# A hybrid decoder layer on one core: the last two experts scattered singly by products of 64 rows, ten loads of one unit, and a final norm by whole blocks

## The chip, the core and the metric

The kernel runs on one core of a Trainium2 chip. The metric is the device time of one execution in microseconds; each figure is the median of several runs. Engines are named as in the profile: PE (TensorE, matrix products) with its weight loads PEld, DVE (VectorE), ACT (ScalarE), POOL (GpSimd), SP (SyncE, which here issues nearly all DMAs).

## The reference

One layer, batch 1, 256 tokens of width 1024, all in float32. It is cut here to what bears on the change, which lies wholly in the expert part and the final norm.

```
def moe_ffn(x, w_router, b_router, w_gu, b_gu, w_down, b_down):
    logits = (x @ w_router + b_router)
    top_vals, top_idx = lax.top_k(logits, TOP_K)          # 4 of 32
    top_w = jax.nn.softmax(top_vals, axis=-1)
    gates = jnp.sum(jax.nn.one_hot(top_idx, N_EXPERTS) * top_w[..., None], axis=1)
    def expert(acc, params):
        wgu_e, bgu_e, wd_e, bd_e, gate_e = params
        h = x @ wgu_e + bgu_e                              # 1024 -> 2048
        hg, hu = h[:, :D_FF], h[:, D_FF:]
        hg = jnp.minimum(hg, 7.0); hu = jnp.clip(hu, -7.0, 7.0)
        act = (hu + 1.0) * (hg * jax.nn.sigmoid(1.702 * hg))
        return acc + gate_e[:, None] * (act @ wd_e + bd_e), None

h = x + (attention heads | Conformer convolution) @ w_out
h = h + moe_ffn(rmsnorm(h, norm_ffn_g), ...)
out = rmsnorm(h, norm_final_g)      # y = h * rsqrt(mean(h*h) + 1e-6) * g
```

## The kernel before

The first tenth of the time is attention, convolution, output projection and routing. Then come 32 experts in a loop that is unrolled, and at last the norm.

**Weights.** An expert has 12 units of 1 MB: 8 of `w_gu` (up projection, 128 input rows each) and 4 of `w_down` (256 rows each, two rows of 1024 numbers on each partition). They lie in a ring of 22 units in SBUF. `SEQUENCE` gives their order: expert by expert, but for the last two experts (numbers 30 and 31) first all up units of 30, all up units of 31, then the down units of 30, then those of 31. `load_sizes` packs them into DMAs: four units mostly; from expert 30 on (`FINE_FROM`) two, and the very last two singly. SP issues a load as soon as PE has counted `units_used` up far enough to free its place, and PE waits on a semaphore of `load_full` for each load, at its first unit.

**One expert.** For each expert up to 64 of the 256 tokens are gathered (`gather`) by products with a 0/1 matrix. `up` multiplies them with the up units; an output of 64 rows takes half of the array's columns, so the two halves of each weight row go side by side (128\*64 in the profile). DVE and ACT make the activation (`expert_pass`, `gate_sigmoid`), PE turns it (`turn_act`), `down` multiplies with the down units. The result is 64 tokens by 1024, held in PSUM as two halves of 512 columns one above the other: partitions 0 to 63 the first half, 64 to 127 the second.

**Scattering.** Experts go in pairs. The results of the even one are copied to partitions 0 to 63 of `y_sb`, those of the odd one to 64 to 127 (`copy_results`). DVE writes each token's gate in a matrix (`weigh_tokens`), PE turns it (`turn_weights`), ACT copies it to `scatter_sb` (`copy_scatter`), and `scatter(buffer, t, h)` adds a pair's results to the block of 128 tokens t and half of columns h of `resid`, which lies in PSUM; these are four products of 128 rows for each pair, spread over the next two experts. For the last pair nothing comes behind: `last_expert` runs `up`, two scatters of the pair before with `turn_weights` between them, the down projection of expert 30 with `turn_act` of 31 in its middle, then that of 31. Behind it ACT and DVE copy one half each, and all four scatters follow.

**The norm.** For each block and each half, ACT squares and sums (L557), DVE multiplies with the gain (L1161) and makes the mean of the two sums in two small steps (L1165, L1168), ACT takes the root, DVE the reciprocal (L1172). The scaling of block 0 is POOL's, in two halves (L547); that of block 1 is DVE's (L1176) and ACT's (L800). SP issues four stores in the order (0,0), (0,1), (1,0), (1,1). There is a path for experts with over 64 tokens (`extra`); the inputs used here don't take it.

The order of each engine's work is the program's text; engines meet by semaphores alone.

## Time and profile before

| | us |
|---|---|
| median of 3 runs | 1042.81 |
| lowest, highest | 1042.51, 1043.61 |
| span of the profiled execution, first to last instruction | 1041.7 |
| PE busy | 1000.4 (96%) |
| DVE busy | 238.4 (23%) |
| ACT busy | 144.9 (14%) |
| POOL busy | 16.5 (2%) |
| HBM read | 419.82 MB, 404 GB/s over the span |

The profiled execution's time by the clock of the runs is not listed apart; its span stands 1.1 us below the median of the runs. In the profile a float32 product appears as two records, so four products are "x8". Matmul records overlap each other: from the start of one row to the start of the next is a better measure than the sum of the durations. L1182 is the line of the helper that issues every product; what a row does is told by its tiles: `work<-ring,main` is up or down projection, `work<-select,main` gathering, `resid<-main` scattering, L1538 turning an activation, L1496 turning weights. A bracket at the end is the idle time in front and what ended it.

### The profile page before, as it was taken

What the parts mean: (1) busy time and instruction counts of PE and PEld (TensorE: products, weight loads), DVE (VectorE), ACT (ScalarE), POOL (GpSimd) and SP (SyncE); (2) the same over time, 40 slices, a digit from 0 to 9 for tenths busy, and PEclk for the clock granted to TensorE, in tenths of its full rate; (3) what the DMA queues carried; (4) which work ended last, traced back from release to release, by engine and by line L of the source; (5) the groups of instructions that cost most, each with busy time, mean ns of one, the idle gap of its engine ahead of it and who ended that gap; (6) DMA issues with size and microseconds to landing.
All of it is one profiled execution on the core that took longest, in us unless ns stands there. A gap on an engine that the chain in (4) does not pass through costs nothing.

```text
span 1041.7 us, 12870 instructions
## 1 busy us (share of the span) xinstructions
PE 1000.4 (96%) x5774; PEld 411.0 (39%) x5775; DVE 238.4 (23%) x535; ACT 144.9 (14%) x277; POOL 16.5 (2%) x28
## 2 busy tenths in 40 slices
PE   9999999999999999999999999899999999999996
PEld 7875544333333333333333333332333333323332
DVE  3995341111011111111111111110111111101121
ACT  5144320100000101010101001000101001000102
POOL 4000000000000000000000000000000000000001
PEclk9999999999999999999999999999999999999999
DMA  9995599999999999999999999999999999999993
GB/s 308 392 414 195 214 397 399 416 418 424 430 424 434 429 433 427 431 427 435 425 433 427 433 427 433 427 435 428 428 433 427 432 430 430 432 428 426 425 424 161
DMA packets 33381, 421.75 MB, mean 405 GB/s; under 512 B 4031, under 2 KB 8427, under 8 KB 14380
## 3 DMA queue, kind: packets, MB, share of 16 engines
q1 hardware_dynamic: 31772, 420.57, 96.0%
q8 instruction: 47, 0.77, 0.3%
q10 hardware_dynamic: 1552, 0.33, 0.2%
q14 instruction: 10, 0.08, 0.0%
HBM read 419.82 MB, written 1.05 MB: 404 GB/s over the span
## 4 chain that ended last, share of the span: by engine, by line
PE 62%; DMA 36%; DVE 1%; issue 1%; POOL 0%; POOLq 0%; ACT 0%; SPq 0%; DVEq 0%
PE work L1182 53%; DMA ring<-in_w_gu 32%; PE resid L1182 7%; DMA ring<-in_w_down 4%; PE work L1538 1%; PE work L1298 0%; PE work L1496 0%; PE work L1397 0%; POOLq L148 0%; DVE main L938 0%; POOL main L547 0%; PE work L1208 0%; DVE ring L837 0%; DVE main L918 0%; DVE main L1161 0%
## 5 line engine op out<-in xcount | busy, mean ns | idle before, releaser
L1182 PE MATMUL work<-ring,main 128*64 128x512 f32 (+1 forms) x3080 | 685.3, 598 | 28.7 <-DMA ring<-in_w_gu 25.8
L1182 PEld LDWEIGHTS work<-ring,main 128*64 128x64 f32 (+1 forms) x3080 | 222.3, 139 | 472.4 <-issue 431.5
L1091 DVE TENSOR_SCALAR main<-work 128x512 f32<-128x512 f32 x32 | 22.1, 691 | 582.7 <-PE work L1182 582.7
L734 ACT ACTIVATE main<-main 128x512 f32<-128x512 f32 x32 | 20.2, 631 | 459.0 <-DVE main L1091 459.0
L1182 PE MATMUL work<-ring 128*128 128x256 f32 (+2 forms) x308 | 71.9, 403 | 1.8 <-DVE ring L837 0.9
L1182 PE MATMUL resid<-main 128*128 128x512 f32 x128 | 68.1, 618 | 0.9 <-DVE main L1153 0.9
L1182 PE MATMUL work<-bgu_rows,ident 128*64 128x512 f32 (+1 forms) x260 | 62.4, 599 | 0.0
L1182 PEld LDWEIGHTS work<-ring 128*128 128x128 f32 (+1 forms) x308 | 55.6, 186 | 16.4 <-issue 8.3
L1182 PEld LDWEIGHTS work<-select,main 128*128 128x128 bf16 x1536 | 46.7, 98 | 26.6 <-issue 26.3
L748 ACT ACTIVATE main<-work 64x512 f32<-64x512 f32 x63 | 37.2, 591 | 118.7 <-PE work L1182 117.9
L1182 PE MATMUL work<-select,main 128*128 128x64 bf16 x1536 | 50.7, 193 | 0.1
L1084 DVE TENSOR_SCALAR lent<-count,place,gates 128x64 f32<-128x64 f32 x64 | 16.9, 308 | 146.9 <-PE work L1496 139.1
L884 DVE SCALAR_TENSOR_TENSOR main<-ring,main 128x256 f32<-128x256 f32 x116 | 46.6, 478 | 1.3 <-ACT main L609 1.2
L739 ACT ACTIVATE main<-work 128x512 f32<-128x512 f32 x32 | 19.1, 597 | 115.1 <-PE work L1538 115.1
L1098 DVE SCALAR_TENSOR_TENSOR main<-main 128x512 f32<-128x512 f32 x32 | 34.1, 1067 | 1.1
L1182 PEld LDWEIGHTS resid<-main 128*128 128x128 f32 x128 | 19.4, 189 | 27.4 <-issue 27.4
L1182 PE MATMUL resid<-ring,main 128*128 128x512 f32 (+1 forms) x68 | 28.8, 571 | 0.0
L1095 DVE TENSOR_TENSOR main<-main 128x512 f32<-128x512 f32 x32 | 22.2, 693 | 5.4 <-ACT main L734 5.4
L1182 PEld LDWEIGHTS work<-bgu_rows,ident 128*64 128x64 f32 x260 | 15.6, 135 | 19.4 <-issue 17.7
L1538 PEld LDWEIGHTS work<-ident,main 128*128 128x128 f32 x128 | 15.8, 141 | 17.9 <-issue 17.0
L745 ACT ACTIVATE main<-work 128x256 f32<-128x256 f32 x16 | 6.1, 383 | 114.7 <-PE work L1496 114.7
L1092 DVE TENSOR_SCALAR main<-work 128x512 f32<-128x512 f32 x32 | 21.8, 680 | 0.0
(190 smaller groups left out, 275.0 us busy)
## 6 DMA issues: line engine op xcount, KB each, us to landing
ring<-in_w_gu SPq DMA_DIRECT2D x36, 4096.0 KB, 41.8
ring<-in_w_gu SPq DMA_DIRECT2D x36, 2048.0 KB, 17.1
ring<-in_w_down SPq DMA_DIRECT2D x18, 4096.0 KB, 43.5
ring<-in_w_gu SPq DMA_DIRECT2D x8, 3072.0 KB, 37.7
ring<-in_w_down SPq DMA_DIRECT2D x11, 2048.0 KB, 15.7
ring<-in_w_down SPq DMA_DIRECT2D x20, 1024.0 KB, 14.3
ring<-in_w_gu SPq DMA_DIRECT2D x15, 1024.0 KB, 27.6
ring<-in_w_down SPq DMA_DIRECT2D x4, 3072.0 KB, 40.0
```

The source lines that it names most:

```text
L734: nc.scalar.activation(sig_h, gate_h, ACT.Sigmoid, scale=SWIGLU_ALPHA).then_inc(sig_ready, 1)
L739: nc.scalar.activation(to, work[:, act_bank(n), :], ACT.Copy).then_inc(act_t_ready, 1)
L745: nc.scalar.activation(scatter_sb[buffer][0:rows, :], work[0:rows, TURN_BANK, 0:TB * P], ACT.Copy).then_inc(scatter_ready, 1)
L748: return nc.scalar.activation(y_sb[buffer][h][parity * CAP:(parity + 1) * CAP, :], work[h * CAP:(h + 1) * CAP, bank, :], ACT.Copy)
L884: V.scalar_tensor_tensor(acc, u_pad[:, c, j:j + SEQ], dw_cols[:, c, j:j + 1], acc, ALU.mult, ALU.add)\
L1084: done = V.tensor_scalar(weighted[:, t, parity * CAP:(parity + 1) * CAP], count[:, bass.ds(r * CAP, CAP)], place[:, t, bass.ds(e, 1)], gat ...
L1091: V.tensor_scalar(gate_h, work[:, GATE_BANK, :], SWIGLU_LIMIT, None, ALU.min).then_inc(gate_clamped, 1)
L1092: V.tensor_scalar(up_h, work[:, UP_BANK, :], SWIGLU_LIMIT, -SWIGLU_LIMIT, ALU.min, ALU.max).then_inc(up_clamped, 1)
L1095: V.tensor_tensor(sig_h, sig_h, gate_h, ALU.mult).then_inc(glu_ready, 1)
L1098: V.scalar_tensor_tensor(gate_h.rearrange("p (b j) -> p j b", b=4), up_h.rearrange("p (j b) -> p j b", b=4), 1.0, sig_h.rearrange("p (j b) ...
L1182: return nc.tensor.matmul(out_, lhsT, rhs, start=start, stop=stop, skip_group_check=True)
L1538: last = nc.tensor.transpose(work[:, act_bank(n), j * P:(j + 1) * P], gate_h[:, j * P:(j + 1) * P], ident[:, :])
```

## The change

Four things change, all from the last two experts on.

1. **Loads.** From unit 374 on (the last two up units of expert 31 and all eight down units of 30 and 31) each load is one unit. The very last unit is split in two DMAs, one for each of its two rows, with a semaphore for the second (`last_row_in`).
2. **Scattering singly.** Experts 30 and 31 each have a scatter matrix of their own. DVE writes the same weights in both halves of the matrix (`weigh_tokens` with parity 0 and 1), so that after the turn they stand on partitions 0 to 63 and on 64 to 127. The result is copied as it lies, one copy of 128 partitions by ACT, and `scatter_alone` adds it in products of 64 rows: half h of the columns from partitions 64h to 64h+63. There are four such products for each of the two experts. DVE's copy of one half is gone.
3. **Order on PE.** The scatters of the pair before and the turn of weights go in the middle of the last up projection; a second turn of weights goes behind `turn_act` in the middle of expert 30's down projection; expert 30's four scatters go behind the first unit of expert 31's down projection.
4. **Norm.** ACT squares 1024 columns at once and takes the root with scale 1/1024 and the epsilon as bias (from a column that POOL sets at the start). Half 0 of each block is multiplied with the gain first and scaled afterwards (POOL for block 0, ACT for block 1); half 1 is done by DVE in one instruction for both factors. The stores go in the order (0,1), (0,0), (1,1) from SP, and (1,0) from ACT's own queue.

PE behind the fourth up unit of expert 31. `resid<-main` are the scatters, L1496 (after: L1508) the turn of weights, `load_full` the loads' semaphores. Before:

```order
L1182 MATMUL work<-ring,main 64x512 [waits load_full3]
L1182 MATMUL work<-ring,main 64x512 x7
L1182 MATMUL resid<-main 128x512 [waits scatter_ready,act_t_ready]
L1496 MATMUL work<-ident,lent 128x128 [waits weighted_ready]
L1496 MATMUL work<-ident,lent 128x128
L1182 MATMUL resid<-main 128x512
L1182 MATMUL work<-ring,main 64x512 [waits load_full4,act_t_ready]
L1182 MATMUL work<-ring,main 64x512 x7
```

and now:

```order
L1188 MATMUL work<-ring,main 64x512 [waits load_full1]
L1188 MATMUL work<-ring,main 64x512 x7
L1188 MATMUL resid<-main 128x512 [waits scatter_ready,act_t_ready]
L1188 MATMUL resid<-main 128x512
L1508 MATMUL work<-ident,lent 128x128 [waits weighted_ready]
L1508 MATMUL work<-ident,lent 128x128
L1188 MATMUL work<-ring,main 64x512 [waits load_full2]
L1188 MATMUL work<-ring,main 64x512 x7
```

The four instructions that stood behind the eighth up unit stand behind the fourth, and the two scatters are next to each other.

PE in the last down projection, expert 31's. Before, from its first unit to the end of its fourth and the first scatters:

```order
L1182 MATMUL work<-ring,main 64x512 [waits load_full6,act_t_ready]
L1182 MATMUL work<-ring,main 64x512 x7
L1182 MATMUL work<-ring,main 64x512 [waits load_full7]
L1182 MATMUL work<-ring,main 64x512 x3
L1182 MATMUL work<-ring,main 64x512 [waits load_full8]
L1182 MATMUL work<-ring,main 64x512 x3
L1182 MATMUL resid<-main 128x512 [waits y_ready,scatter_ready]
L1182 MATMUL resid<-main 128x512 [waits y_last]
L1182 MATMUL resid<-main 128x512 x2
```

and now, from behind its first unit:

```order
L1188 MATMUL resid<-main 128x512 [waits y_ready]
L1188 MATMUL resid<-main 128x512 x3
L1188 MATMUL work<-ring,main 64x512 [waits load_full10]
L1188 MATMUL work<-ring,main 64x512 x3
L1188 MATMUL work<-ring,main 64x512 [waits load_full11]
L1188 MATMUL work<-ring,main 64x512 x3
L1188 MATMUL work<-ring,main 64x512 [waits load_full12]
L1188 MATMUL work<-ring,main 64x512
L1188 MATMUL work<-ring,main 64x512 [waits last_row_in]
L1188 MATMUL work<-ring,main 64x512
L1188 MATMUL resid<-main 128x512 [waits y_ready,scatter_ready]
L1188 MATMUL resid<-main 128x512 x3
```

Four scatters of expert 30 stand between the first unit and the second (their rows read 128x512 by their output; they take 64 rows in), each unit has its own wait, the last one two, and the four scatters at the end wait once.

DVE in the final norm; L1161 (after: L1170) is the product with the gain. Before:

```order
L1161 TENSOR_TENSOR main<-resid,ring 128x512 [waits o_squared,final_gain_in]
L1165 TENSOR_SCALAR stat<-stat 128x1
L1168 TENSOR_SCALAR stat<-stat 128x1 [waits o_squared,o_mean]
L1161 TENSOR_TENSOR main<-resid,ring 128x512 [waits o_squared]
L1172 RECIPROCAL stat<-stat 128x1 [waits o_root]
L1161 TENSOR_TENSOR main<-resid,ring 128x512 [waits o_squared,o_scale]
L1165 TENSOR_SCALAR stat<-stat 128x1
L1168 TENSOR_SCALAR stat<-stat 128x1 [waits o_squared,o_mean]
L1161 TENSOR_TENSOR main<-resid,ring 128x512 [waits o_squared]
L1172 RECIPROCAL stat<-stat 128x1 [waits o_root]
L1176 TENSOR_SCALAR main<-main,stat 128x512 [waits o_gained,o_scale]
```

and now:

```order
L1170 TENSOR_TENSOR main<-resid,ring 128x512 [waits o_squared,final_gain_in]
L1175 RECIPROCAL stat<-stat 128x1 [waits o_root]
L1177 SCALAR_TENSOR_TENSOR main<-resid,stat,ring 128x512 [waits o_scale]
L1170 TENSOR_TENSOR main<-resid,ring 128x512 [waits o_squared]
L1175 RECIPROCAL stat<-stat 128x1 [waits o_root]
L1177 SCALAR_TENSOR_TENSOR main<-resid,stat,ring 128x512 [waits o_scale]
```

Eleven instructions become six; the two on single columns are gone, and half 1 is read from PSUM by one instruction with both factors.

The diff, without semaphore declarations, the waits on the constants, the path for full experts and the last counts:

```diff
+    ALONE_FROM, LAST_UNIT = UNITS * E - 10, UNITS * E - 1
...
-                sizes.append(1 if n >= UNITS * E - 2 else 2)
+                sizes.append(1 if n >= ALONE_FROM else 2)
...
+                    if first == LAST_UNIT:
+                        halves_ = ring_rows(first, size, from_.shape[1])
+                        sp.dma_start(halves_[:, 0, :], from_[:, 0, :]).then_inc(load_full[k % LOAD_SEMS], 16)
+                        sp.dma_start(halves_[:, 1, :], from_[:, 1, :]).then_inc(last_row_in, 16)
+                        continue
...
-            for n in range(HALVES):
-                t, half = n // 2, slice(n % 2 * HALF, (n % 2 + 1) * HALF)
-                if n < 2:
-                    sp.wait_ge(result_ready, n + 1)
-                else:
-                    sp.wait_ge((last_ready, last_half_ready)[n - 2], 1)
+            for t, h, made in ((0, 1, (last_ready, 1)), (0, 0, (result_ready, 1)), (1, 1, (last_ready, 2))):
+                half = slice(h * HALF, (h + 1) * HALF)
+                sp.wait_ge(*made)
...
+            def last_expert(e):
+                copy_scatter(PAIRS - 1, 1, P, (PAIRS - 2) * HALVES)
+                gate_sigmoid(e)
+                copy_act(e)
+                copy_scatter(PAIRS, 0, P, (PAIRS - 1) * HALVES)
+                act.wait_ge(units_used, downs_used(e - 1))
+                nc.scalar.activation(alone_y[0], work[:, OUT_BANK, :], ACT.Copy).then_inc(y_ready, 1)
...
-            copy_half((E - 1) // 2 % 2, (E - 1) % 2, 1, UP_BANK).then_inc(y_last, 1)
+            nc.scalar.activation(alone_y[1], work[:, UP_BANK, :], ACT.Copy).then_inc(y_ready, 1)
...
+            act.wait_ge(consts_ready, 6)
             for t in range(TB):
-                for h in range(2):
-                    act.wait_ge(scattered, total * (HALVES * (SEQ // CAP - 1)) + (HALVES * (PAIRS - 1) + 2 * t + h + 1))
-                    mean_square(resid[:, t, h * HALF:(h + 1) * HALF], work[:, GATE_BANK + h, :],
-                                stat[:, 2 * t + h:2 * t + h + 1], o_squared)
-                act.wait_ge(o_mean, 2 * t + 2)
-                nc.scalar.activation(stat[:, 8 + t:9 + t], stat[:, 6 + t:7 + t], ACT.Sqrt).then_inc(o_root, 1)
-                if t == TB - 1:
-                    act.wait_ge(o_scale, TB)
-                    act.wait_ge(o_gained, HALVES)
-                    nc.scalar.activation(result[:, t, HALF:D], result[:, t, HALF:D], ACT.Copy, scale=stat[:, 10 + t:11 + t])\
-                        .then_inc(last_half_ready, 1)
+                act.wait_ge(scattered, total * (HALVES * (SEQ // CAP - 1)) + (SCATTERS - HALVES + 2 * t + 2))
+                mean_square(resid[:, t, :], work[:, GATE_BANK:GATE_BANK + 2, :].rearrange("p h n -> p (h n)"), stat[:, t:t + 1], o_squared)
+                act.wait_ge(o_squared, t + 1)
+                nc.scalar.activation(stat[:, 8 + t:9 + t], stat[:, t:t + 1], ACT.Sqrt, scale=1.0 / D, bias=eps_col[:, :]).then_inc(o_root, 1)
+            act.wait_ge(o_gained, 2)
+            act.wait_ge(o_scale, TB)
+            nc.scalar.activation(result[:, 1, 0:HALF], result[:, 1, 0:HALF], ACT.Copy, scale=stat[:, 11:12]).then_inc(last_half_ready, 1)
+            act.wait_ge(last_half_ready, 1)
+            act.dma_start(out[0, P:2 * P, 0:HALF], result[:, 1, 0:HALF]).then_inc(result_out, 16)
...
+                if e >= E - 2:
+                    weigh_tokens(e, 0, 0, PAIRS - 1 + e - (E - 2))
+                    weigh_tokens(e, 0, 1, None)
+                elif e > 1:
...
-            V.tensor_copy(y_sb[(E - 1) // 2 % 2][0][CAP:P, :], work[0:CAP, UP_BANK, :]).then_inc(y_ready, 1)
...
-            def gained(t, h):
-                half = slice(h * HALF, (h + 1) * HALF)
-                dve.wait_ge(o_squared, 2 * t + h + 1)
-                V.tensor_tensor(result[:, t, half], resid[:, t, half], final_gain[:, half], ALU.mult).then_inc(o_gained, 1)
-            for t in range(TB):
-                gained(t, 0)
-                V.tensor_scalar(stat[:, 4 + t:5 + t], stat[:, 2 * t:2 * t + 1], 1.0 / D, RMS_EPS, ALU.mult, ALU.add).then_inc(o_mean, 1)
-                dve.wait_ge(o_mean, 2 * t + 1)
-                dve.wait_ge(o_squared, 2 * t + 2)
-                V.tensor_scalar(stat[:, 6 + t:7 + t], stat[:, 2 * t + 1:2 * t + 2], 1.0 / D, stat[:, 4 + t:5 + t], ALU.mult, ALU.add)\
-                    .then_inc(o_mean, 1)
-                gained(t, 1)
-                dve.wait_ge(o_root, t + 2)
+            def gained(t):
+                dve.wait_ge(o_squared, t + 1)
+                V.tensor_tensor(result[:, t, 0:HALF], resid[:, t, 0:HALF], final_gain[:, 0:HALF], ALU.mult).then_inc(o_gained, 1)
+            def finished(t):
+                dve.wait_ge(o_root, t + 1)
                 V.reciprocal(stat[:, 10 + t:11 + t], stat[:, 8 + t:9 + t]).then_inc(o_scale, 1)
                 dve.wait_ge(o_scale, t + 1)
-                if t == TB - 1:
-                    dve.wait_ge(o_gained, 2 * t + 1)
-                    V.tensor_scalar(result[:, t, 0:HALF], result[:, t, 0:HALF], stat[:, 10 + t:11 + t], None, ALU.mult).then_inc(last_ready, 1)
+                V.scalar_tensor_tensor(result[:, t, HALF:D], resid[:, t, HALF:D], stat[:, 10 + t:11 + t], final_gain[:, HALF:D],
+                                       ALU.mult, ALU.mult).then_inc(last_ready, 1)
+            for t in range(TB):
+                gained(t)
+                finished(t)
...
+            def scatter_alone(buffer, y, t):
+                for h in range(2):
+                    rows = slice(h * CAP, (h + 1) * CAP)
+                    mm(resid[:, t, h * HALF:(h + 1) * HALF], scatter_sb[buffer][rows, t * P:(t + 1) * P], y[rows, :], False, False).then_inc(scattered, 1)
...
+                        if n == LAST_UNIT and b == 1:
+                            pe.wait_ge(last_row_in, 16)
...
-                pair, before = e // 2, (e // 2 + 1) % 2
-                up(e, e)
-                pe.wait_ge(act_t_ready, e)
-                pe.wait_ge(scatter_ready, pair)
-                scatter(before, 1, 0)
-                pe.wait_ge(weighted_ready, e + 1)
-                turn_weights()
-                scatter(before, 1, 1)
-                down(e - 1, e - 1, between=lambda: turn_act(e))
-                down(e, e)
+                def during_up():
+                    pe.wait_ge(act_t_ready, e)
+                    pe.wait_ge(scatter_ready, PAIRS - 1)
+                    scatter(0, 1, 0)
+                    scatter(0, 1, 1)
+                    pe.wait_ge(weighted_ready, E)
+                    turn_weights()
+                def during_other_down():
+                    turn_act(e)
+                    pe.wait_ge(scatter_ready, PAIRS)
+                    pe.wait_ge(weighted_ready, E + 2)
+                    turn_weights()
+                def during_down():
+                    pe.wait_ge(y_ready, E - 1)
+                    for t in range(TB):
+                        scatter_alone(1, alone_y[0], t)
+                up(e, e, between=during_up)
+                down(e - 1, e - 1, between=during_other_down)
+                down(e, e, between=during_down, between_at=1)
...
-            scatter((PAIRS - 1) % 2, 0, 0)
-            pe.wait_ge(y_last, 1)
-            scatter((PAIRS - 1) % 2, 0, 1)
-            for h in range(2):
-                scatter((PAIRS - 1) % 2, 1, h)
+            for t in range(TB):
+                scatter_alone(0, alone_y[1], t)
```

## Rows read from the trace of the kernel before

**Rows 1.** Page, sections 1 and 2: engine shares, and GB/s in 40 slices.
```profile
PE 1000.4 (96%) x5774; PEld 411.0 (39%) x5775; DVE 238.4 (23%) x535; ACT 144.9 (14%) x277; POOL 16.5 (2%) x28
...
GB/s 308 392 414 195 214 397 399 416 418 424 430 424 434 429 433 427 431 427 435 425 433 427 433 427 433 427 435 428 428 433 427 432 430 430 432 428 426 425 424 161
```

**Rows 2.** Windows of 59 us: busy us by engine, granted clock, DMA share, GB/s.
```profile
830.00:889.00 59.00, 53.24 (x312) 19.57 (x312) 8.76 (x18) 5.20 (x9) 0.00 (x0) 0.97 1.00 428
...
959.00:1018.00 59.00, 58.92 (x344) 21.43 (x340) 11.48 (x20) 4.94 (x9) 0.00 (x0) 1.00 1.00 424
```

**Rows 3.** Timeline of PE, last 64 us: start us, us, engine, line, operation, count.
```profile
977.96 13.95 PE L1182 MATMUL work<-ring,main 128*64 128x512 f32 x64
...
997.57 14.26 PE L1182 MATMUL work<-ring,main 128*64 128x512 f32 x64
1011.75 1.12 PE L1182 MATMUL resid<-main 128*128 128x512 f32 x2
1012.72 0.38 PE L1496 MATMUL work<-ident,lent 128*128 128x128 f32 x2
1012.93 1.02 PE L1182 MATMUL resid<-main 128*128 128x512 f32 x2
1013.89 3.65 PE L1182 MATMUL work<-ring,main 128*64 128x512 f32 x16
1017.47 0.66 PE L1538 MATMUL work<-ident,main 128*128 128x128 f32 x4
1018.06 3.65 PE L1182 MATMUL work<-ring,main 128*64 128x512 f32 x16
1022.99 7.09 PE L1182 MATMUL work<-ring,main 128*64 128x512 f32 x32 [1.28 <-DMA ring<-in_w_down]
1030.95 3.67 PE L1182 MATMUL resid<-main 128*128 128x512 f32 x8 [0.87 <-DVE main L1153]
```

**Rows 4.** Timeline of PE's weight loads at two waits for data.
```profile
1018.05 0.20 PEld L1182 LDWEIGHTS work<-ring,main 128*64 128x64 f32 x4 [0.17 <-DMA ring<-in_w_down]
...
1027.82 0.14 PEld L1182 LDWEIGHTS work<-ring,main 128*64 128x64 f32 x2 [0.33 <-DMA ring<-in_w_down]
```

**Rows 5.** Timeline of DVE: last expert's activation, then the final norm.
```profile
1014.05 1.07 DVE L1098 SCALAR_TENSOR_TENSOR main<-main 128x512 f32<-128x512 f32 x1
1030.12 0.68 DVE L1153 COPY main<-work 64x512 f32<-64x512 f32 x1 [15.00 <-PE work L1182]
1032.87 0.69 DVE L1161 TENSOR_TENSOR main<-resid,ring 128x512 f32<-128x512 f32 x1 [2.07 <-ACT work L557]
...
1034.46 0.15 DVE L1172 RECIPROCAL stat<-stat 128x1 f32<-128x1 f32 x1
```

**Rows 6.** Timeline of ACT in the final norm.
```profile
1032.08 0.58 ACT L557 ACTIVATE work<-resid 128x512 f32<-128x512 f32 x1 [0.49 <-PE resid L1182]
1032.58 0.20 ACT L557 ACTIVATION_READ_ACCUMULATOR work<-resid 128x1 f32 x1
```

**Rows 7.** Timeline of POOL in the final norm.
```profile
1034.71 3.11 POOL L547 TENSOR_SCALAR main<-main,stat 128x512 f32<-128x512 f32 x2 [910.35 <-DVE stat L1172]
```

**Rows 8.** Timeline of SP: the last two stores issued.
```profile
1038.24 0.94 SPq L487 DMA_DIRECT2D result<-main  x2
```

**Rows 9.** Groups by form, PE: busy us, mean ns of one.
```profile
L1182 PE MATMUL resid<-spare,lent 32*128 32x512 f32 x8 | 3.7, 600 | 0.0
```

**Rows 10.** Groups by form, ACT.
```profile
L557 ACT ACTIVATE main<-main 128x1024 f32<-128x1024 f32 x1 | 1.1, 1057 | 9.2 <-DVE main L1019 9.2
```

**Rows 11.** Groups by form, DVE.
```profile
L970 DVE SCALAR_TENSOR_TENSOR main<-main,stat 128x1024 f32<-128x1024 f32 x1 | 1.3, 1285 | 1.3 <-ACT main L694 1.3
...
L970 DVE SCALAR_TENSOR_TENSOR main<-main,stat 128x384 f32<-128x384 f32 x2 | 1.1, 610 | 0.0
```

**Rows 12.** DMA issues: KB each, median us from issue to landing.
```profile
result<-main SPq DMA_DIRECT2D x4, 256.0 KB, 2.4
...
spare<-in_b_down ACTq DMA_DIRECT2D x1, 128.0 KB, 6.9
```

More of the change, by code:

```diff
@@ L500, in _ @@
             nc.gpsimd.memset(ones_b[:, :], 1.0).then_inc(consts_ready, 1)
+            nc.gpsimd.memset(eps_col[:, :], RMS_EPS).then_inc(consts_ready, 1)
             nc.gpsimd.memset(ident_b[:, :], 0.0).then_inc(consts_step, 1)
@@ L771, in extra @@
                 copy_act(o + E)
-                copy_scatter(o + PAIRS, 0, CAP, (o + PAIRS) * HALVES)
+                copy_scatter(o + ALONE_SETS, 0, CAP, (o + ALONE_SETS) * HALVES)
                 copy_results(o * UNITS + downs_used(E), 0, 0)
                 nc.scalar.activation(stat[:, 13:14], stat[:, 14:15], ACT.Sqrt)
-            for e in range(E):
+            for e in range(E - 1):
                 expert(e)
@@ L1511, in extra_bias, with up @@
                     mm(work[:, bank, :], extra_sel[:, bank, :, :].rearrange("p h c -> p (h c)"), bgu_rows[:, :], True, False)
-            def up(g, e, o=None):
+            def up(g, e, o=None, between=None):
                 if not (isinstance(g, int) and g == 0):
@@ L1517, in up @@
                 for kb in range(KB):
+                    if kb == KB // 2 and between is not None:
+                        between()
                     if isinstance(g, int) and g == 0:
@@ L1539, in turn_act, with down @@
                 last.then_inc(act_turned, 1)
-            def down(g, e, o=None, between=None):
+            def down(g, e, o=None, between=None, between_at=DOWN_UNITS // 2):
                 pe.wait_ge(act_t_ready, g + 1)
@@ L1544, in down @@
                 for u in range(DOWN_UNITS):
-                    if u == DOWN_UNITS // 2 and between is not None:
+                    if u == between_at and between is not None:
                         between()
@@ L1640, in _ @@
             last_expert(E - 1)
-            pe.wait_ge(scatter_ready, PAIRS)
+            pe.wait_ge(scatter_ready, PAIRS + 1)
             pe.wait_ge(y_ready, E)
-            scatter((PAIRS - 1) % 2, 0, 0)
-            pe.wait_ge(y_last, 1)
-            scatter((PAIRS - 1) % 2, 0, 1)
-            for h in range(2):
-                scatter((PAIRS - 1) % 2, 1, h)
+            for t in range(TB):
+                scatter_alone(0, alone_y[1], t)
             def extra(e, r, o):
```

36 lines of the change are left out of this document (17 added, 19 removed).

## The prediction, made before the changed kernel ran

> **What bounds the kernel now.** I read the page first: TensorE counts as busy for 96% of the span, and the weights arrive at about 430 GB/s in nearly every slice, so the two are close [rows 1]. Windows of 59 us come next. One near the middle of the expert loop has 53.2 us of TensorE work and a full DMA stream; the one before the end has 58.9 us of work and a full stream [rows 2]. So the stream sets the pace of the loop, but in the last two experts TensorE has hardly any slack of its own. The change touches only this end, so I then went along TensorE's timeline through its last 64 us [rows 3]. The granted clock is 1.00 in that last window and 0.97 in the other; the sum below holds at 1.00.
>
> There the reader is to see three things. The last expert's up projection begins at 997.57. From there to 1030.08 (the end of the last down product, 1022.99 + 7.09) TensorE works on without a break except for about 0.3 us inside the 14.26 us stretch (8 units at the rate of 13.95 for 8), 0.17 us before 1018.05 [rows 4], and 1.28 us before 1022.99, where it waits for a load of two units. And the last unit's data is waited for once more, until 1027.82 [rows 4], the very moment when TensorE comes to it (its weights are loaded just ahead of 1022.99 + 3 x 1.74 = 1028.2): in this run both limits meet there. Behind 1030.08 comes a serial tail: copies of the result, four scatter products (1030.95 to 1034.62) [rows 3], the norm, and stores. POOL normalises both halves of block 0 in 3.11 us, until 1037.82 [rows 7]; SP issues stores in program order, so block 1's two stores, ready earlier, are issued only behind it, the last at 1039.18 minus half of 0.94, about 1038.71 [rows 8]. The span ends 2.52 us after 1039.18. That tail of 11.6 us from 1030.08 is where time can be had.
>
> Span here is 1041.7, the median of three runs 1042.81: about 1.1 lies around the span, and I keep that.
>
> **The change part by part.**
>
> *Loads.* Units land one by one in the slowest queue's time: a two-unit load is waited for at 1022.99 and the last unit lands at 1027.82, two units later, so 2.4 us a unit. With single units the wait of 1.28 goes, and so do the 0.17 and the 0.3: by the landings so counted every unit is there at least 0.8 us before TensorE's new schedule (below) wants it. The last unit comes as two rows. If data were the limit, half a unit of products would be left behind 1027.82: 2.26 us (to 1030.08) less half of 1.74, so the last product would end at 1029.2. This is the floor. Smaller loads cost stream time: between windows with four-unit and with two-unit loads the rate falls from 428 to 424 GB/s [rows 2], 0.55 us in 59 us for about six more loads, 0.09 us each. The change has five more (four pairs split, one unit split): about 0.5 us at that price, none to several us as outer bounds. It moves the floor to 1029.7 and is hidden as long as TensorE is later than that. The norm's gain load queues behind them as before; it isn't needed until the norm.
>
> The Trainium skill speaks against small loads: "DMA: Bandwidth & Descriptors", section "Anatomy of one DMA", gives a fixed cost of about 2.0 us a transfer beside its bytes. By that rule in series, five loads more would cost 10 us, an estimate from that page. The trace's 0.09 us a load says that with many loads queued it is not paid in series; rival 2 takes it up.
>
> *TensorE's order.* A unit of products takes 13.95/8 = 1.74 us. Before, 2.14 us (1011.75 to 1013.89) of other-expert scatters and weight turns stand behind the up projection; they move into its middle. That alone costs TensorE nothing but makes the activations of the last expert later by that much: up ends at 997.57 + 6.98 + 2.14 + 6.98 = 1013.67. The down projection of the last but one starts at once; two units take 3.58 (1013.89 to 1017.47), so 1017.25. DVE and ACT need 3.37 us from the end of up to the activation (1011.75 to 1014.05 + 1.07 = 1015.12) [rows 3, 5]: 1017.04, so turning it is not waited for, with 0.2 us in hand. Turning: 0.42 (1017.47 to 1018.06 without the 0.17), and new, a second turn of weights, 0.21 (1012.72 to 1012.93). 1017.88. Two units more and the last expert's first: 5.23, so 1023.11. ACT's copy of the other expert's result (0.6 us) is hidden by that first unit.
>
> *Four scatter products of 64 rows each in the middle.* No row shows products on 64 rows. The nearest: products that share the array by columns, 128\*64, take 13.95 us for 64 records, 0.22 each, whereas full ones take 3.67 for 8, 0.43 steady [rows 3]; so pairs overlap by columns. A product with only 32 rows and no partner is no cheaper than a full one, 600 ns mean [rows 9]. Bounds: 1.71 + 0.12 for a change of shape (0.97 us between 1011.75 and 1012.72 against two records at 0.43) = 1.83 if both row halves run together; 3.54 if they don't. The two halves use different rows and write different banks of PSUM, like the column pairs in independence, so I take 1.83: 1024.94. The last three units, and the drain, take 7.09 - 1.74 = 5.35: the last down product ends at **1030.3**, 0.2 later than before, above the floor of 1029.7. What was waiting has been filled by the new work.
>
> The Trainium skill agrees: "TensorEngine Tiling (Array Packing)", section "Key Properties", has tiles work in parallel, but says that changing the tiling mode drains the engine. No row here prices that for row tiles; two drains of the kind seen at 1012.72 are in the sum, 0.1 each.
>
> *Behind it.* One ACT copy of 128x512 (0.58 for such a block [rows 6]) in place of two copies of 64x512 side by side, DVE's 0.68 being the later [rows 5]: the gap of 0.87 becomes 0.79. The scatter starts at P = 1031.1. As row pairs, block 0 is whole after 1.13 us (as one full product before: 1030.95 to 1032.08) and block 1 after 1.98.
>
> *The norm.* ACT squares 1024 columns at once: 0.58 + 0.43 (1.06 for 1024 columns [rows 10]), sum read at 1.13 instead of 0.70 (1032.08 to 1032.78 [rows 6]). It gives the sum of both halves at once, and the mean, epsilon and root in one ACT instruction, where DVE had two small ones and a hop. From ACT's start: DVE's product with the gain at 1.22 (0.09 hop, 32.78 to 32.87), 0.69 long; reciprocal 0.15 [rows 5]; then one scalar_tensor_tensor on 512 columns. It lies between 0.61 (384) and 1.285 (1024) [rows 11]: 0.61 + 128 x 1.05 ns = 0.75. That is at 2.81. ACT's second block: start at 1.38 (root taken as long as the accumulator read, 0.20), sum at 2.51, seen at 2.60, so DVE is the later. The second round takes 0.69 + 0.15 + 0.75 = 1.59: done at 4.40, or P + 5.53, issue at P + 5.57. Before it was 1038.71 - 1030.95 = 7.76. POOL has one half instead of two: 1.56 from P + 3.2 on, P + 4.8, so it is no longer last; SP issues it between the two others.
>
> *The stores.* The last two are issued at once, from SP and from ACT: 0.47 + 2.52 as before. SP's stores land in 2.4 us, and the nearest load issued by ACT, in the middle of the weight stream, in 6.9 [rows 12]. By these bounds the last store could cost 0 to 4.5 us more; idle engines at the end make me take 0, and keep 0.5 as usual error.
>
> *Sum.* 1031.1 + 5.57 + 0.47 + 2.52 = 1039.7, against 1041.7: terms +0.2 (TensorE), -0.1 (copy), -2.2 (scatter to last issue). The time: 1042.81 - 2.0 = **1040.8**. One added memset of POOL (0.1 us) at the start is hidden by the loads.
>
> **The rivals.**
> 1. *Row halves don't overlap.* Price 1.71 for each set of four. The middle set makes the last down product end at 1032.0. Behind it, block 0 is whole at 1.98, block 1 at 3.69; DVE starts block 1 at 3.69 + 1.22 = 4.91, issue at 6.54. End: 1032.0 + 0.79 + 6.54 + 2.99 = 1042.3, time 1043.4, slower than before by 0.6 us. For it: rows 9, and weight loads of full width that must be hidden in 0.43. Against: the column pairs. It decides from about three quarters of that price on.
> 2. *Single loads slow the stream.* TensorE ends 1.1 us above the floor of 1029.2, so up to 0.22 us for each of the five loads nothing is seen; from 0.63 us each (3.1 us) the whole gain is lost. The dearest that rows allow: a store of 256 KB takes 2.4 us from issue to landing [rows 12], of which its bytes at 428 GB/s are 0.6, so 1.8 us apart from them; five times in series the stream ends 9 us later, and the span at 1047.5 (9 more than in rival 3), time 1048.6. The rates of rows 2 speak against it. By the skill's 2.0 us a transfer it would be 10 us instead of 9.
> 3. *The stream is the limit, not TensorE.* If the new work costs less or starts earlier than I count, the last product ends at the floor: 1029.2 + 0.79 + 5.57 + 2.99 = 1038.5, time 1039.6. For it: the wait of 1.28 was real; against: TensorE's sum above leaves no slack.
>
> **How the numbers follow.** A run of this kernel tells about 0.2%, 2.1 us, from no change. Forecast, 0.66: 1040.8, own range 1040.0 to 1041.8. Rival 1, 0.20: 1043.4. Rival 2, 0.04. Rival 3, 0.10. Faster by over 0.2% (below 1040.7): 0.42 of the forecast's, which stands on that bound, and 0.9 of rival 3: 0.37. Slower by over 0.2% (above 1044.9): most of rival 2 and a sixth of rival 1 (a store of ACT's that lands late on top): 0.06. The rest, 0.57, is no change that can be measured. Range: 1039.3 to 1043.6, from rival 3 to rival 1 with a margin.
>
> **What would show it.** TensorE: records of 64-row products on resid eight at a time in about 1.9 us; if 3.5, rival 1. No wait for in_w_down over 0.2 us behind 1013; the last down product's end about 0.2 to 0.3 us later than 1030.08, and a last unit landed well before it. Between the last down product and the last issue 6.4 us instead of 8.6. POOL busy once with 1.56 us in the norm. The forecast is wrong if the last weights land later than 1029, if turning the last activation is waited for, or if ACT's store ends over 0.5 us behind SP's.

## The result, and the profile after

The changed kernel is slower: 1044.45 us median of 20 runs (1042.68 to 1046.07) against 1043.03 us of the kernel before (20 runs, 1042.00 to 1044.21). The ratio is 1.0015, interval 1.0009 to 1.0021. The forecast was 1040.8, the range ended at 1043.6.

| | before | after |
|---|---|---|
| median of 20 runs, us | 1043.03 | 1044.45 |
| spread (standard deviation), us | 0.6 | 1.0 |
| span of the profiled execution, us | 1041.7 | 1041.1 |
| that execution's time, us | not listed | 1042.87 |

The profiled execution of the changed kernel is the second lowest of its 20 runs, 1.6 us below their median. Time and span lie 1.7 to 1.9 us apart in every run where both are known, so the profiled execution of before, span 1041.7, took about 1043.4 (an estimate), some 0.6 above the 1042.81 on which I had put my sum. Both matter below.

TensorE's timeline of the changed kernel, from one expert further back than [rows 3] (columns: start us, us, then engine, line, operation, tiles, count, idle time before):

```profile
957.77 7.09 PE L1188 MATMUL work<-ring,main 128*64 128x512 f32 x32 [0.81 <-DMA ring<-in_w_gu]
...
1004.53 1.99 PE L1188 MATMUL resid<-main 128*128 128x512 f32 x4
...
1006.66 10.52 PE L1188 MATMUL work<-ring,main 128*64 128x512 f32 x48
1017.11 0.66 PE L1552 MATMUL work<-ident,main 128*128 128x128 f32 x4
...
1017.92 5.37 PE L1188 MATMUL work<-ring,main 128*64 128x512 f32 x24
1023.22 1.99 PE L1188 MATMUL resid<-main 64*128 64x512 f32 x8
1025.14 5.37 PE L1188 MATMUL work<-ring,main 128*64 128x512 f32 x24
1031.30 1.99 PE L1188 MATMUL resid<-main 64*128 64x512 f32 x8 [0.79 <-ACT main L796]
```

From the wait of 0.81 us before 957.77 to the end of the last down product at 1025.14 + 5.37 = 1030.51 there is no wait for data any more; 8 records of 64 rows take 1.99 us where 8 of 128 rows took 3.67 [rows 3]. The last down product ends 0.4 us later than before (1030.08), not 0.2 as forecast. The tail after that, all engines (ACT's copy, ACT's square, DVE's first product, POOL, SP's and ACT's store issues):

```profile
1030.55 0.60 ACT L796 ACTIVATE main<-work 128x512 f32<-128x512 f32 x1 [6.82 <-PE work L1188]
...
1032.47 1.01 ACT L564 ACTIVATE work<-resid 128x1024 f32<-128x1024 f32 x1 [1.32 <-PE resid L1188]
...
1033.68 0.69 DVE L1170 TENSOR_TENSOR main<-resid,ring 128x512 f32<-128x512 f32 x1 [16.63 <-ACT work L564]
...
1034.63 1.57 POOL L554 TENSOR_SCALAR main<-main,stat 128x512 f32<-128x512 f32 x1 [910.12 <-DVE stat L1175]
...
1035.26 1.79 SPq L495 DMA_DIRECT2D result<-main  x3
...
1036.74 0.39 ACTq L810 DMA_DIRECT2D result<-main  x1
```

Each step lies within 0.2 us of the sum: first scatter at 1031.30 (1031.1 forecast), last issue at 1036.74 (1036.67). But the span ends 4.4 us after that issue, where the prediction had 3.0 from [rows 8]. The stores' issues with KB and median us to landing:

```profile
result<-main SPq DMA_DIRECT2D x3, 256.0 KB, 2.7
result<-main ACTq DMA_DIRECT2D x1, 256.0 KB, 4.0
```

### The profile page after: what moved, and what is told of

It reads as the page before. It is cut to its first block, busy times and chain, and to the rows that moved or that the text cites. A ratio compares the mean times of both kernels' runs of the same rounds, so it can differ in the third digit from the quotient of the medians.

```text
span 1041.1 us, 12883 instructions
## 1 busy us (share of the span) xinstructions
PE 1000.6 (96%) x5784; PEld 411.0 (39%) x5785; DVE 237.7 (23%) x533; ACT 144.3 (14%) x272; POOL 14.9 (1%) x28
## 4 chain that ended last, share of the span: by engine, by line
PE 65%; DMA 32%; DVE 1%; issue 0%; SPq 0%; ACT 0%; DVEq 0%; ACTq 0%
PE work L1188 56%; DMA ring<-in_w_gu 32%; PE resid L1188 7%; PE work L1552 1%; DMA ring<-in_w_in 1%; PE work L1508 0%; PE work L1304 0%; PE work L1403 0%; DVE main L947 0%; SPq L378 0%; DVE main L927 0%; DVE main L1170 0%; ACT work L564 0%; SPq L375 0%; DVE main L1177 0%
## 5 line engine op out<-in xcount | busy, mean ns | idle before, releaser
L1188 PE MATMUL resid<-main 128*128 128x512 f32 (+1 forms) x136 | 68.3, 618 | 0.8 <-ACT main L796 0.8
L1188 PEld LDWEIGHTS resid<-main 128*128 128x128 f32 (+1 forms) x136 | 19.5, 189 | 28.1 <-issue 28.1
```

The source lines that it names most:

```text
L1188: return nc.tensor.matmul(out_, lhsT, rhs, start=start, stop=stop, skip_group_check=True)
```

## The experiments

Every experiment ran in 11 runs beside 33 of the kernel before on the same chip. Three theories: **S**, the store from ACT's queue is late; **P**, TensorE has no slack left at the end, so that a delay inside the last 70 us goes through to the end; **L**, the single loads slow the stream.

| run | median us | spread | before | ratio to before (interval) |
|---|---|---|---|---|
| e1 changed kernel again | 1044.03 | 1.1 | 1042.85 | 1.0013 (1.0004 to 1.0022) |
| e2 all stores from SP | 1043.69 | 0.9 | 1042.85 | 1.0007 (0.9998 to 1.0016) |
| e3 loads in pairs | 1044.42 | 0.9 | 1042.85 | 1.0015 (1.0006 to 1.0024) |
| e4 scatter behind the last down | 1041.41 | 1.1 | 1042.85 | 0.9991 (0.9982 to 1.0000) |
| e5 pairs from expert 27 on | 1043.24 | 0.4 | 1043.02 | 0.9999 (0.9990 to 1.0008) |
| e6 before + norm and stores | 1042.52 | 0.4 | 1043.02 | 0.9994 (0.9985 to 1.0003) |
| e7 before + single loads | 1042.91 | 0.9 | 1043.02 | 0.9995 (0.9986 to 1.0004) |
| e8 e4 + e5 | 1041.77 | 0.4 | 1043.02 | 0.9985 (0.9976 to 0.9994) |
| e9 before + pairs from 27 on | 1043.51 | 0.6 | 1043.26 | 1.0001 (0.9992 to 1.0010) |
| e10 e8 with pairs at the end | 1042.60 | 0.4 | 1043.26 | 0.9995 (0.9986 to 1.0004) |
| e11 e4 + pairs from unit 352 on | 1041.46 | 0.4 | 1043.26 | 0.9983 (0.9974 to 0.9992) |
| e12 before + loads, norm, pairs from 352 | 1041.47 | 0.6 | 1043.26 | 0.9983 (0.9974 to 0.9992) |

### e1: the changed kernel again

No edit.

> The changed kernel once more, to get a second profile and the spread beside kernels that differ in one thing. Theory S (the store from ACT's queue): median 1.0 to 2.0 us above the kernel before, and the last store again lands about 4 us after its issue where SP's land in 2.2 to 2.7. Theory P (TensorE has no slack left at the end): the last up and down products run without a wait from 957 on, and a stretch at the lower clock there lengthens the span by as much as it lasts, where the kernel before absorbed it. Theory L (single loads slow the stream): the last unit lands later than 1027.8 by over 1 us.

1044.03 us, 1.2 above the kernel before; the result stands. Its profile fell on the fastest of its 11 executions (1042.78, span 1041.0) and runs like the first.

### e2: all four stores from SP

```diff
-            for t, h, made in ((0, 1, ...), (0, 0, ...), (1, 1, (last_ready, 2))):
+            for t, h, made in ((0, 1, ...), (0, 0, ...), (1, 1, (last_ready, 2)), (1, 0, (last_half_ready, 1))):
-            act.wait_ge(last_half_ready, 1)
-            act.dma_start(out[0, P:2 * P, 0:HALF], result[:, 1, 0:HALF]).then_inc(result_out, 16)
```

> The changed kernel with the one store of ACT's queue issued by SP instead, fourth and last. Theory S: 1.0 to 1.5 us faster than e1, so close to or below the kernel before, and the last store lands within 2.7 us. Theory P and theory L: within 0.4 us of e1 (SP's issue is 0.4 us later, the landing the same).

0.3 us below e1, which their intervals can't tell from nothing. The profile settles it: with all four stores from SP the span still ends 4.1 us after the last issue, so ACT's queue as such isn't the cause and theory S falls. This profile fell on the slowest of the 11 executions, 1045.01. TensorE's timeline, at the two last waits for a load of four units:

```profile
928.63 7.09 PE L1186 MATMUL work<-ring,main 128*64 128x512 f32 x32 [2.30 <-DMA ring<-in_w_gu]
...
958.20 8.79 PE L1186 MATMUL work<-ring,main 128*64 128x512 f32 x32 [2.63 <-DMA ring<-in_w_gu]
```

At 958.20, 32 records take 8.79 us, which took 7.09 at the same place of the changed kernel's first profile. The windows of this kernel around it (us, busy of PE, PEld, DVE, ACT, POOL, then granted clock, DMA share, GB/s):

```profile
955.00:957.00 2.00, 0.57 (x4) 0.00 (x0) 0.00 (x0) 0.00 (x0) 0.00 (x0) 1.00 1.15 492
957.00:960.00 3.00, 1.80 (x6) 0.69 (x8) 0.00 (x0) 0.00 (x0) 0.00 (x0) 0.76 0.95 407
960.00:965.00 5.00, 5.00 (x20) 1.50 (x18) 0.00 (x0) 0.00 (x0) 0.00 (x0) 0.80 1.01 433
965.00:970.00 5.00, 5.00 (x66) 2.37 (x62) 2.76 (x4) 0.63 (x1) 0.00 (x0) 1.00 0.97 410
```

and the same of the changed kernel's first profile:

```profile
957.00:960.00 3.00, 2.23 (x12) 0.80 (x14) 0.00 (x0) 0.00 (x0) 0.00 (x0) 1.00 0.99 426
960.00:965.00 5.00, 5.00 (x31) 1.62 (x28) 0.09 (x1) 0.00 (x0) 0.00 (x0) 1.00 0.99 423
```

In e2 TensorE idles 2.6 us, and then the granted clock is 0.76 and 0.80 of full: for a while it works at the lower of its two levels (1.2 instead of 2.4 GHz). That costs 1.7 us, and every later row stands about 2 us later than in the profile of the changed kernel, to the last scatter (1033.42 against 1031.30), since nothing waits in between.

Such a stretch is nothing special to e2. From 570 us on, each of the 14 profiles, the kernel before included, has four or five sets of 32 records of 8.4 to 8.8 us, each behind a wait of 1.9 to 2.8 us for a load of four units. What differs is where they fall. The kernel before:

```profile
870.25 8.78 PE L1182 MATMUL work<-ring,main 128*64 128x512 f32 x32 [2.00 <-DMA ring<-in_w_gu]
...
899.40 7.09 PE L1182 MATMUL work<-ring,main 128*64 128x512 f32 x32 [0.75 <-DMA ring<-in_w_gu]
...
928.60 8.78 PE L1182 MATMUL work<-ring,main 128*64 128x512 f32 x32 [1.99 <-DMA ring<-in_w_gu]
...
957.83 7.09 PE L1182 MATMUL work<-ring,main 128*64 128x512 f32 x32 [0.83 <-DMA ring<-in_w_gu]
```

and the changed kernel's first profile at the third of these places:

```profile
928.57 8.79 PE L1188 MATMUL work<-ring,main 128*64 128x512 f32 x32 [2.01 <-DMA ring<-in_w_gu]
```

Behind a stretch of 8.8 us the wait for the next load of four units is 0.75 and 0.83 us here; where the stretch is missing (e2 at 928.63) it is 2.63. The wait gives back what the stretch cost, and the products behind it start at nearly the same time either way (957.77 and 958.20). At 957 no long wait is left behind, so there a stretch goes through to the end. The changed kernel's first profile is a good one because its last stretch fell at 928.57 and not at 957. This is theory P's mechanism, seen.

### e3: the ten loads in pairs

```diff
-                sizes.append(1 if n >= ALONE_FROM else 2)
+                sizes.append(1 if n >= UNITS * E - 2 else 2)
```

and the last unit in one DMA.

> The changed kernel with the loads of the kernel before (two units each, the last two single, no split unit). Theory L: faster than e1 by 1 us or more. Theories S and P: within 0.5 us of e1, or slower by up to 0.5 where a pair is waited for. In the trace, waits of TensorE for in_w_down of up to 1.3 us if the pairs matter, none if TensorE comes later than the data anyway.

No gain (1044.42), so theory L falls as a cause of the miss. Its profile (1044.41) has its last low-clock stretch where e2 has it, 8.78 us for 32 records at 957.52 behind a wait of 2.62, and no wait for `in_w_down` at all: TensorE comes later than its data, singly or in pairs.

### e4: expert 30's scatters behind the last down projection

```diff
-                down(e, e, between=during_down, between_at=1)
+                down(e, e)
+                during_down()
```

> The changed kernel with the four products of 64 rows of expert 30 behind the last down projection, ahead of the wait for ACT's copy, not in its middle. Theory P: the last down product ends 1.9 us earlier unless data is the limit (then 1.1 to 1.3 us), the gap of 0.79 us before the last scatters is filled, and the time falls by 0.8 us against e1. Theories S and L alone: no more than that either; if the time falls by under 0.3 us the end was not bound by TensorE.

```profile
957.69 7.09 PE L1188 MATMUL work<-ring,main 128*64 128x512 f32 x32 [2.51 <-DMA ring<-in_w_gu]
...
1017.84 10.69 PE L1188 MATMUL work<-ring,main 128*64 128x512 f32 x48
1028.45 3.70 PE L1188 MATMUL resid<-main 64*128 64x512 f32 x16
```

1041.41, 2.6 us faster than e1, from moving four products by 5 us. I had expected 0.8. The profile, of the fastest of the 11 executions, has a span 2.0 us below the changed kernel's first: 2.0 us leave the down projection and the last 16 records (3.70 us) run without the gap of 0.79, so the last scatter ends 1.1 us earlier; the other 0.9 lies behind the last issue, in the stores (3.5 us from ACT's issue to the end instead of 4.4). The runs fall in two groups: six at 1040.87 to 1041.41, five at 1042.45 to 1044.02. The means of the groups lie 2.0 us apart, near the 1.7 of a low-clock stretch; that the upper group are the executions with a stretch behind 957 isn't shown, as only one run of the lower group was profiled. (In this profile the wait of 2.51 us isn't followed by one: the wait doesn't always bring it on. Its last stretch is at 899.)

### e5: loads of two units from expert 27 on

```diff
-    SINGLES, FINE_UP_TO, FINE_FROM = (...), UNITS * 8, UNITS * (E - 2)
+    SINGLES, FINE_UP_TO, FINE_FROM = (...), UNITS * 8, UNITS * (E - 5)
```

> The changed kernel with loads of two units already from expert 27 on instead of 30. Theory P: the wait of up to 2.6 us for the last load of four units (at 957 to 958) and the stretch at the lower clock behind it go, TensorE enters the last two experts 1.5 us earlier or more, and the time falls by 1 to 2 us against the changed kernel, with less spread between runs. Theory L (small loads slow the stream): no gain, or a loss of up to 0.5 us.

```profile
953.21 3.65 PE L1188 MATMUL work<-ring,main 128*64 128x512 f32 x16 [1.20 <-DMA ring<-in_w_gu]
958.18 3.65 PE L1188 MATMUL work<-ring,main 128*64 128x512 f32 x16 [1.32 <-DMA ring<-in_w_gu]
...
983.82 3.65 PE L1188 MATMUL work<-ring,main 128*64 128x512 f32 x16 [1.24 <-DMA ring<-in_w_gu]
988.81 3.65 PE L1188 MATMUL work<-ring,main 128*64 128x512 f32 x16 [1.34 <-DMA ring<-in_w_gu]
```

Waits of 1.2 to 1.3 us take the place of one of 2.6. The last low-clock stretch of this profile begins at 840.52. In the four profiles with pairs from expert 27 on (e5, e8, e9, e10) none begins behind 871; of the ten others all but e6 have one at 898.9 or later. No run is above 1043.79 where e1 reached 1046.58, the spread falls from 1.1 to 0.4, and the median by 0.8 us (of 1 to 2 expected). TensorE doesn't enter the last two experts 1.5 us earlier, as expected, but later: it waits for data until 988.81 and ends its last down product at 1031.1, 0.6 later than without, for nine more loads.

### e6: the new norm alone

The kernel before, with the changed kernel's norm and stores (part 4 of the change).

> The kernel before with the new norm and its stores alone. By my sum for the norm: the last two scatters in full rows, then 6.5 us from the first scatter to the last issue instead of 7.8, so 1.3 us faster, if the stores land as before; if four stores close together land 1 to 1.5 us later (as in the changed kernel's profiles, 4.0 us from issue to landing), no gain at all. Theory P says nothing here.

```profile
1022.42 7.09 PE L1172 MATMUL work<-ring,main 128*64 128x512 f32 x32 [0.60 <-DMA ring<-in_w_down]
1030.38 3.67 PE L1172 MATMUL resid<-main 128*128 128x512 f32 x8 [0.87 <-DVE main L1147]
```

From the first scatter (1030.38) to the last issue (1036.84) it is 6.46 us, 6.54 by the prediction's working for full rows, 7.76 before: 1.3 us won. The span ends 4.0 after the issue instead of 3.0. What is left is 0.5 us in the medians, within the interval of no change.

### e7: the single loads alone

The kernel before, with part 1 of the change.

> The kernel before with the ten loads of one unit and the split last unit alone. Theory P: the waits for in_w_down of 0.2 and 1.3 us go, TensorE ends its last down product up to 0.9 us earlier, limited by the last unit's landing; 0 to 0.9 us faster. Theory L: slower than the kernel before by 0.5 us or more.

```profile
1013.74 3.65 PE L1189 MATMUL work<-ring,main 128*64 128x512 f32 x16
...
1017.91 10.52 PE L1189 MATMUL work<-ring,main 128*64 128x512 f32 x48
1029.31 3.67 PE L1189 MATMUL resid<-main 128*128 128x512 f32 x8 [0.88 <-DVE main L1160]
```

The wait of 1.28 [rows 3] is gone, and in this execution the last down product ends at 1028.4. Yet the median is where it was (1042.91): the runs fall in two groups again, five at 1041.37 to 1042.04, six at 1042.91 to 1043.75, and the spread is 0.9 instead of 0.7. The profile is of the lower group; its last low-clock stretch is at 928.66 and the next wait 0.92. That the upper group are executions with a stretch behind 957, which the lost wait of 1.28 no longer takes up, fits theory P but isn't shown.

### e8: both repairs

Edits of e4 and e5.

> Both repairs together: expert 30's scatters behind the last down projection and loads of two units from expert 27 on. Theory P: the sum of both can't be had, since the last unit's landing becomes the limit; 0.3 to 1.5 us faster than the late scatter alone (1041.4), and TensorE waits for in_w_down in the last down projection. If nothing is gained over the late scatter alone, the stream was already the limit there.

```profile
1023.19 1.94 PE L1188 MATMUL work<-ring,main 128*64 128x512 f32 x8 [0.41 <-DMA ring<-in_w_down]
1025.66 3.65 PE L1188 MATMUL work<-ring,main 128*64 128x512 f32 x16 [0.53 <-DMA ring<-in_w_down]
1029.25 3.70 PE L1188 MATMUL resid<-main 64*128 64x512 f32 x16
```

1041.77, spread 0.4. By the medians it isn't faster than e4 (1041.41), and the range I gave was wrong; by the ratios to the kernel before (0.9985 against 0.9991) it is 0.6 us faster, but the intervals overlap. The gain is in the spread. TensorE now waits for `in_w_down` in the last down projection (0.41 and 0.53 us): the stream is the limit, as rival 3 had it, here and in e10 to e12, not in the changed kernel.

### e9: the kernel before with pairs from expert 27 on

Edit of e5, on the kernel before.

> The kernel before with loads of two units from expert 27 on, all else as it was. Theory P: the kernel before has 1.3 to 1.9 us of waits of TensorE behind the place where the clock falls, so it absorbs most of a slow stretch; taking the cause away gains little: 0 to 0.5 us, where it gained 1 us in the changed kernel, and less spread than the 0.6 to 0.7 us of the kernel before. If it gains as much as in the changed kernel, the theory of the lost slack is wrong.

1043.51 against 1043.26, no gain, where the same edit took 0.8 off the changed kernel. The spread is 0.6 as in the kernel before, though I had expected less. The kernel before had 1.3 to 1.9 us of waits behind that place and would lose little by a low-clock stretch. That is theory P's second half: the run agrees with it, but no profile caught the kernel before with a stretch behind 957.

### e10: pairs at the end, with late scatters

Edits of e8 and e3.

> The late scatter and the loads of two units from expert 27 on, with the ten last loads in pairs again as in the kernel before. Theory P: once the scatters are out of the last down projection TensorE comes before its data, so here the single loads count: 0.4 to 1.3 us slower than e8 (1041.8), with a wait of about 1 us for in_w_down in front of the last four units. If it is as fast as e8, single loads are worth nothing anywhere.

```profile
1023.33 7.09 PE L1183 MATMUL work<-ring,main 128*64 128x512 f32 x32 [1.29 <-DMA ring<-in_w_down]
1030.35 3.70 PE L1183 MATMUL resid<-main 64*128 64x512 f32 x16
```

0.8 us slower than e8 by the medians, 0.6 when each is taken against the kernel before on its own chip; in the profiles the last scatters start 1.1 us later, with a wait of 1.29 us before the last four units. So the ten single loads are worth 0.6 to 0.8 us, once TensorE is early enough to wait for them.

### e11 and e12: the best version, with and without single scatters

```diff
-    ... FINE_FROM = (...), UNITS * 8, UNITS * (E - 2)
+    ... FINE_FROM = (...), UNITS * 8, UNITS * (E - 3) + 4
```

on e4 (e11), and on the kernel before with the single loads and the new norm (e12).

> The late scatter with loads of two units only from unit 352 on (the last four up units of expert 29 and its down units), so that the last long wait goes and the stream has 8 loads more instead of 18. Theory P: no run with a slow stretch behind 955, so the lower of the two groups of e4: 1041.0 to 1041.4, with the small spread of e8.

> The kernel before with the ten single loads, the new norm and loads of two units from unit 352 on, but its own scattering and order on TensorE (full rows, both experts together at the end). By the trace of e4, block 0 is whole 2.8 us behind the last down product there; with full rows it is 0.87 + 1.98 = 2.85 us. So scattering singly is worth nothing by itself: within 0.5 us of e11. If e11 is faster by 1 us or more, it is worth something.

Both 1041.5, 1.8 us below the kernel before, ratio 0.9983 (0.9974 to 0.9992). e11 has no run above 1042.03 where e4 has five; its median is just above the 1041.0 to 1041.4 expected. (It has two loads more than e4, not the eight of the expectation, where e8 has nine more.) With seven loads fewer than e8, its `in_w_down` waits end 0.6 us earlier (1025.09 against 1025.66): 0.08 us for each load. e12 ends like this, with the old scatters of both experts at once:

```profile
1025.15 3.65 PE L1179 MATMUL work<-ring,main 128*64 128x512 f32 x16 [0.53 <-DMA ring<-in_w_down]
1029.68 3.67 PE L1179 MATMUL resid<-main 128*128 128x512 f32 x8 [0.88 <-DVE main L1154]
```

Its block 0 is complete 2.85 us after the last down product (gap 0.88, two products 1.97); in e4 it is 2.8. So scattering singly brings nothing by itself. What brings the 1.8 us of e12 is the single loads, the norm and the pairs from unit 352 together: alone, the first gave 0.1 us (e7) and the second 0.5 (e6), neither clear of noise. The first two without the third were not run.

## Why the prediction was wrong

**Right:** the loads (no wait for `in_w_down`); the order on TensorE, each start within 0.2 us; the row halves side by side, 1.92 us for eight records (1023.22 to 1025.14) of 1.83 forecast, so rival 1 falls; the gap of 0.79; the norm, 5.44 us from the first scatter to the last issue, of 5.57. Rival 2 falls too: e7 with the same loads is 0.1 us below the kernel before, and e8 against e11 gives 0.08 us a load, close to the 0.09 of the prediction.

"TensorEngine Tiling (Array Packing)" of the Trainium skill, section "Key Properties", has different tiles work in parallel; the 1.92 us agree. The Trainium skill's page "DMA: Bandwidth & Descriptors", section "Anatomy of one DMA", gives its fixed 2.0 us for transfers on GpSimd's path, while these loads are issued by SP, so the prediction's 10 us in series by that rule applied it beyond its heading; the 0.08 us a load measured here doesn't show it either.

**Wrong,** in three places, which add up to the miss of 3.6 us (1044.45 against 1040.8): 1.6, 1.4 and 0.65. The first two are steps of the mechanism, the third is a size:

1. *"What was waiting has been filled by the new work", at a price of 0.2 us.* In one profile it costs 0.4 (1030.51 against 1030.08). The median lies another 1.6 us above that profiled execution. The waits of 1.3 to 1.9 us were slack: behind a low-clock stretch of 1.7 us a wait is shorter by about as much, and the change put 1.9 us of products into the down projection and left no wait behind 957. Shown: that a later wait takes a stretch up (the kernel before at 870.25 and 928.60), and that in the changed kernel one behind 957 goes through to the last scatter (e2 2.1 us, e3 1.45 us later than the first profile). In keeping with it: e5, whose pairs take the stretch away from the end and 0.8 us off the median, and e9, where the same edit does nothing for the kernel before; and e4, which takes the products out again, though 0.9 of its 2.0 us between the profiles are stores. Not shown: that the whole 1.6 us are this. How many of the 20 executions have a stretch behind 957 isn't known, and the slowest lies 3.2 us above the profiled one, more than one such stretch costs. I had read the granted clock of the last 59 us of one execution (1.00) and taken it for granted, though the window of [rows 2] with 0.97 holds such a stretch, at 870.25. None of my rivals was this one.

2. *The stores, "0.47 + 2.52 as before".* They took 4.4 us from the last issue, 1.4 too many. Two parts. The bytes: I counted from the last issue, but three stores of 256 KB follow each other at about 370 GB/s, 0.7 us each. In the kernel before they were issued from 1037.86 on and the span ended 3.84 later; the changed kernel's three begin at 1036.23, so 1040.1. Five profiles (before, e7, e9, e10, e12) end 3.8 us after the first of the last three issues, though the last of these issues comes 0.5 us behind the first in e10 and 0.9 in the kernel before. An earlier last issue doesn't help if the stores ahead still fill the queue. The other 1.0 us: in the changed kernel a packet of 16 KB, which the profile lists as an instruction fetch, runs on one DMA engine among the stores (queue 8, here from 1037.0 on; queue, packets, MB, share):

```profile
q1 hardware_dynamic: 179, 0.33, 91.0%
q8 instruction: 1, 0.02, 5.7%
```

and at the end nine packets of the last store go one by one, while all other engines are idle:

```profile
DMA packets 11, 0.02 MB, mean 12 GB/s; under 512 B 2, under 2 KB 2, under 8 KB 11
...
q10 hardware_dynamic: 9, 0.02, 2.7%
```

Before, such a packet ran at 1036.4, ahead of the last three stores; in e4 at 1034.4, and its last store landed in 2.6 us:

```profile
result<-main ACTq DMA_DIRECT2D x1, 256.0 KB, 2.6
```

In the ten profiles with the last store on ACT's queue, the time from that store's issue to the end goes with it: 3.2 to 3.5 us in e12, e10 and e4, where the packet starts 1.3 to 1.5 us before the issue; 3.8 to 4.2 in e8, e6, e11 and e1 (1.2 to 0.5 before); 4.4 to 4.5 in the first, e5 and e3 (0.3 to 0.4 behind). That is an association; no run moved the packet alone, so this 1.0 us isn't shown, and whose code it fetches is open.

3. *The base.* "About 1.1 lies around the span" compared one execution's span with other executions' median. Within one execution it is 1.75 for the changed kernel's profile, and 1.7 to 1.9 in every run where both are known; that is 0.65 us.

## What to carry to other kernels

A wait on the busiest engine near the end need not be free time: here such waits took up what varies between executions. Filling them saved nothing in a good execution and cost in others, so first shorten the waits that bring the variation on, then fill the rest. Compare medians and spreads beside the two profiles; and see which of its executions a profile shows.

## What the runs showed of the hardware

- In each of the 14 profiles TensorE's granted clock fell for a few us four or five times behind 570 us (0.76 and 0.80 in e2's windows), costing up to 1.7 us for 32 records. Each time it was behind a wait of 1.9 to 2.8 us for data; after other waits as long (2.51 in e4 at 957.69, 2.52 in e6 at 958.24, 2.54 before at 841.03) it didn't fall, and after waits of 1.2 to 1.3 us it fell in none of these profiles.
- Products of 64 rows on the two halves of the rows, into different PSUM banks, run in pairs: eight float32 records of 512 columns in 1.92 us from start to start.
- One instruction fetch of 16 KB took 0.9 to 1.4 us on its queue; the last store of 256 KB ended later the later this packet came, which is an association.
- Loads of two units instead of four, with many queued, cost the stream 0.08 us for each load more (e8 against e11).
